# Building both one-hot matrices of the expert gates in float32, token by token

## The reference, cut to what matters

```python
hid = jnp.einsum('thkd,td->thk', u_tab[eidx], xb, preferred_element_type=jnp.float32)
act = (jax.nn.gelu(hid, approximate=False) * gate).astype(xb.dtype)
return jnp.einsum('thk,thkd->td', act, v_tab[eidx])
```

## Time and profile before

| what | value |
|---|---|
| median of 3 executions | 4530.71 us (4529.45 to 4531.64) |
| the profiled execution | 4534.9 us |
| its span, first to last instruction | 4533.1 us |
| busy over the span: PE, DVE, ACT, POOL | 3933.8, 2888.6, 1200.9, 1170.1 us |
| mean granted clock of PE | 0.933 |
| gate-matrix groups | about 2095 to 2436 us of the span |

### The profile page before, as it was taken

The page is one execution under the profiler, slowest core; times in us unless marked ns, Lnnn a source line. Parts: engine busy times, 40 slices in busy tenths (PEclk is TensorE's granted clock), DMA queues, the critical chain, the costliest instruction groups (busy, mean ns, idle before and its releaser), DMA issues. The chain is left out here.

```text
span 4533.1 us, 58126 instructions
## 1 busy us (share of the span) xinstructions
PE 3933.8 (87%) x21975; PEld 3713.7 (82%) x21975; DVE 2888.6 (64%) x4993; ACT 1200.9 (26%) x1883; POOL 1170.1 (26%) x704
## 2 busy tenths in 40 slices
PE   4999755759999699994666998999999999999998
PEld 2897544648888599993555998999999999999998
DVE  2001335352222369999997768788878688888884
ACT  2112324121111222224884212222222222222221
POOL 0001000000000122223774223333433244444440
PEclk8999767579999899997998999999999999999999
DMA  2110210011112022211335557777777588788872
GB/s 97 42 42 27 80 25 19 11 42 43 42 42 76 20 63 69 69 62 59 167 148 180 158 167 241 233 229 230 240 238 227 166 254 253 243 247 250 255 243 73
DMA packets 538695, 608.91 MB, mean 134 GB/s; under 512 B 223713, under 2 KB 446865, under 8 KB 534435
## 3 DMA queue, kind: packets, MB, share of 16 engines
q1 hardware_dynamic: 460875, 328.00, 24.5%
q0 software_dynamic: 73728, 268.47, 17.5%
q10 hardware_dynamic: 3936, 10.44, 0.6%
HBM read 535.78 MB, written 71.57 MB: 134 GB/s over the span
## 5 line engine op out<-in xcount | busy, mean ns | idle before, releaser
L2257 DVE TENSOR_TENSOR xn<-xn,ps 128x400 f32<-128x400 f32 x816 | 459.5, 570 | 274.8 <-PE ps L79 274.7
L77 PE MATMUL ps<-x_act_high,x_v_high 128*128 128x400 f32 x1664 | 574.5, 345 | 15.2 <-DVE xn L2257 11.4
L77 PE MATMUL ps<-hn_high,x_u_high 128*128 128x400 f32 x1664 | 574.1, 345 | 9.2 <-DVE x_u_low L2188 9.2
L78 PE MATMUL ps<-x_act_low,x_v_high 128*128 128x400 f32 x1664 | 573.4, 345 | 0.0
L79 PE MATMUL ps<-x_act_high,x_v_low 128*128 128x400 f32 x1664 | 573.0, 344 | 0.0
L78 PE MATMUL ps<-hn_low,x_u_high 128*128 128x400 f32 x1664 | 571.6, 343 | 0.0
L79 PE MATMUL ps<-hn_high,x_u_low 128*128 128x400 f32 x1664 | 570.2, 343 | 0.0
L2180 POOL DMA_INDIRECT row_ring<-in_u_rows,row_index x256 | 346.8, 1355 | 573.1 <-DVE row_hid L2214 511.2
L2180 POOL DMA_INDIRECT row_ring<-in_v,row_index x256 | 352.8, 1378 | 509.4 <-DVE row_out L2223 472.2
L77 PEld LDWEIGHTS ps<-x_act_high,x_v_high 128*128 128x128 f32 x1664 | 313.9, 189 | 15.9 <-DVE xn L2257 11.7
L2223 DVE SCALAR_TENSOR_TENSOR row_out<-row_ring,row_hid,row_out 128x1024 f32<-128x1024 f32 x256 | 323.8, 1280 | 0.0
(11 more groups left out here) (349 smaller groups left out, 8109.9 us busy)
## 6 DMA issues: line engine op xcount, KB each, us to landing
xn<-in_u SPq DMA_DIRECT2D x128, 512.0 KB, 4.3
xn<-in_v SPq DMA_DIRECT2D x128, 512.0 KB, 6.0
gates<-gm_out SPq DMA_DIRECT2D x25, 2048.0 KB, 6.3
x_g<-gates SPq DMA_DIRECT2D x52, 800.0 KB, 7.3
wg_raw<-in_w_m SPq DMA_DIRECT2D x24, 512.0 KB, 3.7
kept<-kept_act ACTq DMA_DIRECT2D x24, 400.0 KB, 2.4
k_g<-gates SPq DMA_DIRECT2D x12, 800.0 KB, 7.9
k_act<-kept SPq DMA_DIRECT2D x24, 400.0 KB, 3.2
```

What stands on the lines that cost most here:

```text
L77: pe.matmul(out, w[0], x[0], start=first, stop=False)
L78: pe.matmul(out, w[0], x[1], start=False, stop=False)
L2257: dve.tensor_tensor(m.xd[:, j, a:z], m.xd[:, j, a:z], m.ps[:, 4 + x % 4, 0:DCH], ALU.add).then_inc(added, 1)
```

## The change

Both one-hots are made in the same way: float32, token by token (8 tokens by 128 keys), by comparing the constant row of 0 to 127 with the token's key. The bf16 table `gm_iota` and its construction are gone, the key-2 table is float32, and `gm_hot2` has twice the bytes. POOL weights seven of the eight tokens (896 elements in a partition, read contiguously), ACT one. Waits, buffers, transfers and PE's work are as they were.

```diff
--- before.py
+++ after.py
@@ -1747,11 +1747,10 @@
             return ctx.enter_context(nc.sbuf_tensor(name, shape, dt))
 
 
-        key1, key2, gate = sb("gm_key1", [P, DT]), sb("gm_key2", [P, DT], BF16), sb("gm_gate", [P, DT])
+        key1, key2, gate = (sb(f"gm_{x}", [P, DT]) for x in ("key1", "key2", "gate"))
         turned_in = (key1, key2, gate)
-        iota2 = sb("gm_iota", [P, NK, G8], BF16)
         hot1, wgt = sb("gm_hot1", [P, 2, G8, NK]), sb("gm_wgt", [P, 2, G8, NK])
-        hot2 = sb("gm_hot2", [P, 2, NK, G8], BF16)
+        hot2 = sb("gm_hot2", [P, 2, G8, NK])
         out = sb("gm_out", [P, 2, NK, TBG])
 
         turned, t_kept, hot1_made, hot2_made, weighted, last_weighted, used, copied, base_turned = (
@@ -1790,12 +1789,12 @@
 
             @block.vector
             def _(dve):
-                dve.tensor_copy(iota2[:], iota.unsqueeze(2).broadcast_to([P, NK, G8]))
                 dve.scalar_tensor_tensor(m.rows[:], m.e2[:, 0:NG, :], float(NK), m.e1[:, 0:NG, :], ALU.mult, ALU.add)
                 dve.tensor_copy(m.gate_g[:], m.gate[:, 0:NG, :])
 
 
         GROUPS = TBG // G8
+        BYPOOL = 7
         with nc.Block() as block:
 
             def all_groups(eng, group):
@@ -1814,7 +1813,8 @@
                         dve.wait_ge(weighted, g - 1)
                         dve.wait_ge(last_weighted, g - 1)
 
-                    dve.tensor_tensor(hot2[:, q], iota2[:], key2[:, cols].unsqueeze(1).broadcast_to([P, NK, G8]),
+                    dve.tensor_tensor(hot2[:, q], iota.unsqueeze(1).broadcast_to([P, G8, NK]),
+                                      key2[:, cols].unsqueeze(2).broadcast_to([P, G8, NK]),
                                       ALU.is_equal).then_inc(hot2_made, 1)
                     if not first:
                         dve.wait_ge(used, 2 * (g - 1))
@@ -1827,12 +1827,12 @@
             @block.gpsimd
             def _(pool):
                 def group(g, first, q):
-                    cols = bass.ds(G8 * g, G8 - 2)
+                    cols = bass.ds(G8 * g, BYPOOL)
                     pool.wait_ge(hot2_made, g + 1)
                     if not first:
                         pool.wait_ge(used, 2 * (g - 1))
-                    pool.tensor_tensor(wgt[:, q, 0:G8 - 2], hot2[:, q, :, 0:G8 - 2].rearrange("p n t -> p t n"),
-                                       gate[:, cols].unsqueeze(2).broadcast_to([P, G8 - 2, NK]),
+                    pool.tensor_tensor(wgt[:, q, 0:BYPOOL], hot2[:, q, 0:BYPOOL],
+                                       gate[:, cols].unsqueeze(2).broadcast_to([P, BYPOOL, NK]),
                                        ALU.mult).then_inc(weighted, 1)
 
                 all_groups(pool, group)
@@ -1858,8 +1858,8 @@
                 def weigh(g, q):
 
                     act.wait_ge(hot2_made, g + 1)
-                    for i in (G8 - 2, G8 - 1):
-                        ins = act.activation(wgt[:, q, i], hot2[:, q, :, i], ACT.Copy,
+                    for i in range(BYPOOL, G8):
+                        ins = act.activation(wgt[:, q, i], hot2[:, q, i], ACT.Copy,
                                              scale=gate[:, bass.ds(G8 * g + i, 1)])
                     ins.then_inc(last_weighted, 1)
```

## The result

The changed kernel has a median of 4569.9 us over four executions (4565.19 to 4575.97), against 4531.18 for the kernel before: 1.0085 times, 95% interval 1.0073 to 1.0097. It is slower by 38.7 us, in the direction forecast, where 81.5 us were forecast; the stated range, 4601 to 4630 us, doesn't hold it.

The account below looks back on a forecast made before the run. DVE and POOL holding each other up in turns was taken to bound the gate-matrix stage. 99 rings x 0.815 = 80.7, first one-hot +0.52, last POOL turn +0.285: +81.5 us, forecast 4612 us, range 4601 to 4630.

Parts of the forecast that it names:

- the ring: Gate-matrix stage, per group: key-1 one-hot, POOL after it, remainder of key-2 one-hot; from 3.37 to 4.185 us, +0.815.
- the rest: Gate-matrix stage, from POOL's end to the next key-1 one-hot's start: 0.48 us before, 1.01 forecast, +0.53.
- the key-2 one-hot: DVE in the gate-matrix stage: float32 token by token costs +0.53 us a group; 3.1 us long in steady groups.
- GpSimd's turn: POOL's multiply, from the key-1 one-hot's end to its own: seven tokens instead of six, 1.68 to 1.965 us, +0.285.
- what was costed at nothing: Gate-matrix stage: ACT's saved ACTIVATE, dropped bf16 table, float32 key copy, block stores and PE's clock: 0 us.
- Rival 1: Gate-matrix stage: float32 one-hots don't hold POOL up; POOL 2.125 us, group 2.45 at best, 4440 us; chance 0.02.
- rival 2: Gate-matrix stage: POOL's full 2.125 us follows the key-1 one-hot; 4.345 us a group, about 4628 us; chance 0.08.
- rival 3: Gate-matrix stage: DVE holds POOL up, but POOL doesn't hold float32 one-hots up; at most 3.18 us, 4512; chance 0.01.

Follow-up runs that it names:

- the row in PSUM: Changed kernel with the row of numbers that both one-hots are compared with read from PSUM instead of SBUF: 4425.34 us, 0.9763 against the kernel before.
- float32 key by key: Kernel before with key-2 one-hot, its table and its keys in float32, still key by key, GpSimd six tokens: 4592.99 us, 1.0134.

## Why the prediction was wrong

**Right: the ring.** What bounds the stage was read correctly. In every kernel of the table POOL's turn follows the price of its form by itself, where that was measured, less 0.08 to 0.14 us (what hides that part isn't shown), and the rest is 0.48 or about 1.01 whatever POOL does. That DVE and POOL hold each other up because of two SBUF inputs, which the prediction took from the earlier trace rows, is shown by the row in PSUM. The Trainium skill, SBUF — State Buffer, section Who interferes with whom, says that a DVE instruction with at most one SBUF input outside the 2-port modes doesn't contend: the trace agrees (POOL 1.69 beside DVE, 1.68 alone). The Trainium skill, Advanced Engine Details and Errata, section Mode Summary, names the 2p modes alone; that rule, weighed in the prediction, doesn't describe this kernel, where the `tensor_tensor` one-hots take turns with POOL as long as both inputs lie in SBUF.

**Right: the key-2 one-hot.** +0.53 in the ring (rest 1.01 for 0.48) and 1.23 us in the first group; it ends 1.08 us after POOL (2255.06 + 2.70 = 2257.76), as forecast. That either half of the change, the token order or float32, costs DVE its pace by itself (1.23 us for the first one-hot in both runs), the prediction didn't see; it made no difference to the sum.

**Wrong: GpSimd's turn, forecast at +0.285 and measured at -0.14.** Two errors lie in one step. The price of float32 elements was taken from POOL lines with two full operands; with a gate spread over 128 columns an element costs 1.67 ns and not 2.09, and the whole at 896 is 1.68 and not 2.12. And from that too high price the step concluded that "the source is contiguous float32 and no longer bf16 at a stride of 8 gives nothing": it compared 1.71 by the float32 row with the 1.68 of now. The two agreed only because one had a dear second operand and the other a dear first one. By the forms alone the layout gives 0.315 and the seventh token takes 0.215; in the ring it is 0.35 and 0.21, which is the -0.14. The bounds of the term (1.95 and 1.98) came from two rows of the same kind, so they were narrow around a shared error. 99 x (0.285 + 0.14) = 42 us is nearly the whole miss of 81.5 - 38.7 = 42.8 us. The Trainium skill, SBUF — State Buffer, in the box on cachelines under Door 1: The DMA port swizzle, says that accesses which leave a 16-byte line pay; the source before had 16 bytes from one element to the next, and the trace agrees in kind (1.78 against 1.47); no run here tries a shorter step, so where the price begins isn't shown. The prediction didn't bring that rule in.

**Right: what was costed at nothing.** ACT's saved ACTIVATE, the table, the key copy, the stores: the ring and its two ends account for the 38.7 us, and nothing is left for these. PE's clock, too: in the run with float32 key by key the mean granted clock from 2200 to 2300 us was 0.86. PE had idled for 1.95 us before the pass at 2252.13 and for 1.55 before the one at 2256.13; this second pass took 3.78 us with the clock at 0.50, its level of 1.2 GHz, and the next pass still started on the ring's 4.0 us. The windows (columns as in the earlier trace rows) and the passes:

```profile
2200.00:2300.00 100.00, 60.64 (x400) 55.17 (x400) 100.00 (x51) 70.70 (x101) 66.24 (x26) 0.86 0.30 126
2256.00:2260.00 4.00, 3.78 (x16) 3.49 (x16) 4.00 (x3) 2.02 (x3) 2.64 (x1) 0.50 0.92 389
```

```profile
2252.13 2.45 PE L1850 MATMUL ps<-gm_wgt,gm_hot 128*128 128x128 f32 x16 [1.95 <-ACT gm_out L1871]
2256.13 3.78 PE L1850 MATMUL ps<-gm_wgt,gm_hot 128*128 128x128 f32 x16 [1.55 <-ACT gm_out L1871]
2260.11 2.20 PE L1850 MATMUL ps<-gm_wgt,gm_hot 128*128 128x128 f32 x16 [0.20 <-issue]
```

**The rivals.** None of the three happened. Rival 1's test, POOL near 2.1 us beside a one-hot, had the same wrong price in its 2.125: undisturbed, POOL takes 1.68. It took 2.42, of which 0.88 is the wait for the key-1 one-hot (2255.14 - 2254.26). Against rival 2, POOL ends 1.54 us after that one-hot, less than its whole 1.68. Against rival 3, the group is 3.76 us, above its 3.18, and the key-2 one-hot is stretched from 1.23 us to 2.70 while POOL works.

## What to carry to other kernels

A price goes with the form of an instruction's operands, not with its engine, operation and count: before a row is used for another instruction, compare the access patterns of both inputs, and be wary when two rows that differ in both agree. Where DVE and GpSimd run side by side, look whether DVE's `tensor_tensor` has both inputs in SBUF. Here it had, GpSimd's multiply read SBUF too, and the length of each contained a wait for the other; a constant operand held in PSUM parted them, at 0.9763 of the time of the kernel before. When a ring of turns bounds a stage, work taken off an engine outside the ring and put into it is a loss, however idle the receiver looks: here one token moved from ACT to POOL cost 0.21 or 0.28 us a group.

## What the runs showed that was not expected

- GpSimd's multiply costs 1.67 ns for each further element when the second operand is spread with a step of zero; with a full one 896 elements take 0.387 us more (2.069 against 1.682).
- A source at a stride of 8 elements costs GpSimd 0.315 us (bf16) or 0.395 us (float32) more than a contiguous one for 768 elements; the type of a contiguous source costs it nothing (1.468 and 1.467).
- DVE's one-hot takes as long with a row from PSUM as from SBUF: 1.22 and 1.21 us.
- PE's granted clock was 0.86 in float32 key by key, where PE idled for 1.95 us before a pass of a 4.00 us group, and 0.99 in the changed kernel, with 1.71 us in 3.76. It cost the stage nothing, since PE isn't on the ring.
